# Hybrid encoder block on one core: the two last products with tokens on the partitions, x added as it lies, x2 turned at the second norm

## What is computed

```python
h_in = rms_norm(x, norm1_w)                 # x: (1, 512, 2048)
z = h_in @ w_in                             # attention, RWKV and gate columns
...                                         # o_attn (512 wide), o_rwkv (1024 wide), gates
branch_a = o_attn @ w_branch_attn
branch_b = o_rwkv @ w_branch_rwkv
merged = gates[:, :, 0] * branch_a + gates[:, :, 1] * branch_b
x = x + merged @ w_out                      # output projection and residual: "x2"
h = rms_norm(x, norm2_w)
x = x + (silu(h @ w_ffn_gate) * (h @ w_ffn_up)) @ w_ffn_down    # 5632 hidden channels
```

## Time and profile before

| | us |
|---|---|
| median of 3 runs | 3535.35 |
| lowest and highest run | 3525.96 and 3536.68 |
| the profiled execution | 3531.09 |
| its span in the trace | 3529.4 |
| TensorE busy | 3445.0 |
| VectorE, ScalarE, GpSimd busy | 1593.3, 1112.2, 1685.0 |

### The profile page before, as it was taken

How to read it: one execution, slowest core, us unless ns; L and a number is a source line. 1 busy time by engine, 2 the same in 40 slices (tenths; PEclk the granted TensorE clock), 3 DMA queues, 4 the chain that set the end, 5 groups by cost and what they waited for, 6 DMA issues and landing times.

```text
span 3529.4 us, 43830 instructions
## 1 busy us (share of the span) xinstructions
PE 3445.0 (98%) x16535; PEld 2803.1 (79%) x16535; DVE 1593.3 (45%) x1890; ACT 1112.2 (32%) x1757; POOL 1685.0 (48%) x1429
## 2 busy tenths in 40 slices
PE   8999999999999999999799999999999999999999
PEld 6777777777777888888578878888888888888887
DVE  4455545555567877874344443311331133203321
ACT  4333324444234554553342232211221222112211
POOL 4333333333338888887275434444444444344443
PEclk9999999999999999999899999999999999999999
DMA  6344434433354555553543423333332333333323
GB/s 193 108 137 123 131 116 145 118 113 91 96 154 119 129 127 146 126 133 89 205 138 113 121 88 95 95 90 112 95 95 83 108 95 96 90 103 100 99 85 105
DMA packets 757677, 406.25 MB, mean 115 GB/s; under 512 B 191695, under 2 KB 718219, under 8 KB 757035
## 3 DMA queue, kind: packets, MB, share of 16 engines
q1 hardware_dynamic: 757546, 404.53, 40.3%
HBM read 345.73 MB, written 58.72 MB: 115 GB/s over the span
## 4 chain that ended last, share of the span: by engine, by line
PE 50%; DVE 1%; ACT 0%; DMA 0%; POOL 0%; issue 0%; SPq 0%; DVEq 0%; ACTq 0%; POOLq 0%
PE f_bank L149 15%; PE f_bank L151 15%; PE f_bank L150 15%; PE f_bank L1865 1%; PE f_bank L1866 1%; PE f_bank L1867 1%; DMA act_plain<-yt 0%; PE f_bank L1898 0%; PE f_bank L1874 0%; POOL w_lo_b L140 0%; DVE hid_plain L2322 0%; ACT w_hi_b L133 0%; PE f_bank L1878 0%; DVE act_rounded L2276 0%; PE f_bank L1981 0%
## 5 line engine op out<-in xcount | busy, mean ns | idle before, releaser
L140 POOL TENSOR_TENSOR w_lo_b<-w_raw_b,w_hi_b 128x2048 fp32r<-128x2048 f32 (+1 forms) x168 | 684.7, 4076 | 925.0 <-ACT w_hi_b L133 925.0
L149 PE MATMUL f_bank<-act_rounded,w_lo_b 128*128 128x512 f32 x1664 | 648.6, 390 | 9.1 <-DVE act_rounded L2276 6.6
L150 PE MATMUL f_bank<-act_rounded,w_hi_b 128*128 128x512 f32 x1664 | 648.1, 389 | 0.0
L151 PE MATMUL f_bank<-act_rounded,w_hi_b 128*128 128x512 f32 x1664 | 647.9, 389 | 0.0
L1260 POOL TENSOR_TENSOR ring_w_rounded<-ring_w_plain,ring_w_hi 128x1024 fp32r<-128x1024 f32 x138 | 331.8, 2406 | 626.4 <-ACT ring_w_hi L1273 626.4
L133 ACT CAST w_hi_b<-w_raw_b 128x2048 fp32r<-128x2048 f32 (+1 forms) x168 | 286.4, 1705 | 838.3 <-PE f_bank L151 828.0
L1555 PE MATMUL slab_ps<-h_hi,ring_w_rounded 128*128 128x512 f32 x1088 | 451.4, 415 | 5.1 <-POOL ring_w_rounded L1260 2.6
L1557 PE MATMUL slab_ps<-h_hi,ring_w_hi 128*128 128x512 f32 x1088 | 426.2, 392 | 0.0
L1556 PE MATMUL slab_ps<-h_lo,ring_w_hi 128*128 128x512 f32 x1088 | 426.2, 392 | 0.0
L149 PEld LDWEIGHTS f_bank<-act_rounded,w_lo_b 128*128 128x128 f32 x1664 | 312.6, 188 | 75.4 <-DVE act_rounded L2276 5.3
L151 PEld LDWEIGHTS f_bank<-act_rounded,w_hi_b 128*128 128x128 f32 x1664 | 312.7, 188 | 65.3
(11 more groups left out here) (347 smaller groups left out, 5275.9 us busy)
## 6 DMA issues: line engine op xcount, KB each, us to landing
ring_w_plain<-in_w_in_dram SPq DMA_DIRECT2D x190, 512.0 KB, 4.1
w_raw_b<-in_w_ffn_gate_dram SPq DMA_DIRECT2D x44, 1024.0 KB, 5.2
w_raw_b<-in_w_ffn_up_dram SPq DMA_DIRECT2D x44, 1024.0 KB, 5.1
w_raw_b<-in_w_ffn_down_dram SPq DMA_DIRECT2D x64, 704.0 KB, 4.5
zt<-slab_out SPq DMA_DIRECT2D x65, 256.0 KB, 4.4
w_raw_b<-in_w_out_dram SPq DMA_DIRECT2D x16, 1024.0 KB, 5.5
zt<-lout SPq DMA_DIRECT2D x40, 256.0 KB, 4.6
b_in<-zt SPq DMA_DIRECT2D x80, 128.0 KB, 3.5
```

The lines of the kernel that those rows point to most:

```text
L140: pool.tensor_tensor(g.w_lo[n.slot][:, 0:k, :], g.w_raw[n.slot][:, 0:k, :], g.w_hi[n.slot][:, 0:k, :].bitcast(F32), ALU.subtract).then_inc ...
L149: pe.matmul(bank, wl, hi[:, ka, :], start=start and j == 0, stop=False)
L150: pe.matmul(bank, wh, lo[:, ka, :], start=False, stop=False)
L151: ins = pe.matmul(bank, wh, hi[:, ka, :], start=False, stop=stop and j == len(ks) - 1)
```

## The change

The output projection and the last product swap their operands: the activations (128 channels by 128 tokens) are stationary and the weights (128 by 512 columns) move, so that the result lies with tokens on the partitions. Four banks, one for each 128 tokens, fill together for a group of 512 columns. `outp(q)` counts 16 slabs as before, a slab now being 4 k tiles by 512 columns; `down(b, q)` counts ND = 12 pieces of 4, 4 and 3 k tiles by 512 columns for each of the 4 groups, in place of 16 slabs. Loads of weights have runs of 2 KB, where they had 512 bytes.

x2 is kept in the same buffer, read by `by_tokens(c, t)` as 128 tokens by 512 columns. x is added from eight buffers that SP fills from the input itself. xt, x_turned, `keep`, the 64 unscaled transposes, their copies, the stores and the waits on them are gone, and VectorE and ScalarE share the scaling of x_tok otherwise. The squares are summed by ScalarE along the row (accum_out), and the sum over channels by matmuls is gone. At the second norm TensorE turns x2 (`turn_x2`), four blocks to a tile, into banks 0 to 3: four tiles ahead of the first gate slab, the others between its steps; act_hi and act_lo are made from these banks. At the end x2 is stored as it lies, with no turn and no copy. The loops over slabs of the two products are written out.

```diff
@@ phase_project, SP @@
-                def keep(t):
-                    sp.wait_ge(raw_taken, 4 * t + 4)
-                    sp.dma_start(xt.rearrange("(k p) n -> p k n", p=P)[:, :, t * P:(t + 1) * P], x_turned[t][:, :, :]).then_inc(x_kept[t], 16)
...
-                for t in range(TT):
-                    keep(t)
                 for s in range(N_SLOT + 2):
                     weights(2 * s + 4)
@@ phase_project, ScalarE @@
                 def scale(t):
                     act.wait_ge(rstd_ready, t + 1)
-                    act.wait_ge(raw_turned, 4 * t + 4)
-                    act.activation(x_tok[:, t, D_MODEL // 2:D_MODEL], x_tok[:, t, D_MODEL // 2:D_MODEL], ACT.Copy, scale=rstd[:, t:t + 1]).then_inc(scaled_act, 1)
+                    act.activation(x_tok[:, t, 0:D_MODEL // 2], x_tok[:, t, 0:D_MODEL // 2], ACT.Copy, scale=rstd[:, t:t + 1]).then_inc(scaled_act, 1)
...
-                scale(2)
+                scale(3)
@@ phase_project, VectorE @@
-                scale(1)
-                scale(2)
-                mean_square(3)
-                scale(3)
+                for t in range(1, TT):
+                    mean_square(t)
+                    scale(t)
@@ phase_output, SP @@
+                for q in range(KD):
+                    n = outp(q)
+                    c, i = divmod(q, 4)
+                    sp.wait_ge(g.w_lo_ready, n.count(2))
+                    sp.dma_start(g.w_raw[n.slot][:, :, :].rearrange("p (k j) n -> p k (j n)", j=4),
+                                 w_o[:, 4 * i:4 * i + 4, c * SEQ:(c + 1) * SEQ]).then_inc(g.w_landed[n.slot], 16)
+                    if q == 1:
+                        for n in range(NX):
+                            x_load(n)
+                    elif i == 3 and 1 <= c < 3:
+                        for n in range(4 * c + 4, 4 * c + 8):
+                            x_load(n)
...
-                    sp.dma_start(out[0, t * P:(t + 1) * P, q * SEQ:(q + 1) * SEQ], plain[:, n, :]).then_inc(out_stored, 16)
+                    sp.wait_ge(x2_ready, KD + (NBLK - 1) * KD + n + 1)
+                    sp.dma_start(out[0, t * P:(t + 1) * P, c * SEQ:(c + 1) * SEQ].rearrange("p (m f) -> p m f", f=P), by_tokens(c, t)
+                                 ).then_inc(out_stored, 16)
@@ phase_output, TensorE @@
+                for q in range(KD):
+                    st = outp(q)
+                    c, i = divmod(q, 4)
+                    pe.wait_ge(g.w_lo_ready, st.count())
+                    for kk in range(4):
+                        k = 4 * i + kk
+                        if c == 0:
+                            pe.wait_ge(mlo_ready, k + 1)
+                        wh, wl = by_columns(g.w_hi, st, kk), by_columns(g.w_lo, st, kk)
+                        for t in range(TT):
+                            if k == 0 and c:
+                                pe.wait_ge(x2_ready, 4 * (c - 1) + t + 1)
+                            o, r = bank[4 + t][:, :], slice(t * P, (t + 1) * P)
+                            pe.matmul(o, act_hi[:, k, r], wl, start=k == 0, stop=False)
+                            pe.matmul(o, act_lo[:, k, r], wh, start=False, stop=False)
+                            ins = pe.matmul(o, act_hi[:, k, r], wh, start=False, stop=k == KD - 1)
...
+                for m in range(4):
+                    turn_x2(m)
                 st = gate_up(0, 0, 0)
                 pe.wait_ge(g.w_lo_ready, st.count())
                 for k in range(KD):
                     pe.wait_ge(h2lo_ready, k + 1)
                     ins = products(pe, g, st, [(k, k)], bank[6][:, :], act_hi, act_lo, start=k == 0, stop=k == KD - 1)
+                    if k + 4 < KD:
+                        turn_x2(k + 4)
                 ins.then_inc(g.w_used, 1)
-                pe.wait_ge(sq_added, KD)
-                for t in range(TT):
-                    ins = pe.matmul(bank[4][:, t:t + 1], sq_sum[:, t * P:(t + 1) * P], g.all_ones[:, 0:1], start=True, stop=True)
@@ phase_output, ScalarE @@
                 for k in range(KD):
-                    act.wait_ge(x2_ready, k + 1)
-                    act.activation(act_hi[:, k, :], x2[:, k, :], ACT.Copy, scale=param(g, "norm2", k)).then_inc(h2hi_ready, 1)
-                    if k == 3:
+                    act.wait_ge(turned, k + 1)
+                    act.activation(act_hi[:, k, :], bank[k % 4][:, :], ACT.Copy, scale=param(g, "norm2", k)).then_inc(h2hi_ready, 1)
+                    if k == 7:
                         split_hi(act, g, gate_up(0, 0, 1), KD)
+                    if k == 9:
+                        square_x2(3)
@@ phase_output, VectorE @@
-                    dve.scalar_tensor_tensor(out=act_lo[:, k, :], in0=x2[:, k, :], scalar=param(g, "norm2", k),
+                    dve.scalar_tensor_tensor(out=act_lo[:, k, :], in0=bank[k % 4][:, :], scalar=param(g, "norm2", k),
                                              in1=act_hi[:, k, :].bitcast(F32), op0=ALU.mult, op1=ALU.subtract).then_inc(h2lo_ready, 1)
```

More of the change, by code:

```diff
@@ L1903, in _ @@
                     branch_slab(m)
-                def slabs(step, first, freed, i, K, banks, hi, lo):
-                    for j in range(2):
-                        st = step(i, first + j)
-                        pe.wait_ge(g.w_lo_ready, st.count())
-                        if first:
-                            pe.wait_ge(freed, i * 2 + (j + 1))
-                        products(pe, g, st, [(k, k) for k in range(K)], bank[banks + j][:, :], hi, lo).then_inc(g.w_used, 1)
-                st = outp(0, 0)
@@ L1922, in _, with by_columns @@
-                pe.wait_ge(g.w_lo_ready, st.count())
-                products(pe, g, st, [(k, k) for k in range(KD)], bank[5][:, :], act_hi, act_lo).then_inc(g.w_used, 1)
-                with pe.Fori(0, KD // 2 - 1) as i:
-                    slabs(outp, 2, x2_ready, i, KD, 4, act_hi, act_lo)
+                def by_columns(w, st, i):
+                    return w[st.slot][:, 4 * i:4 * i + 4, :].rearrange("p j n -> p (j n)")
+                for q in range(KD):
[14 more added lines that the diff above has]
+                            ins = pe.matmul(o, act_hi[:, k, r], wh, start=False, stop=k == KD - 1)
+                            if k == KD - 1 and t < TT - 1:
+                                ins.then_inc(made_x2, 1)
+                    ins.then_inc(g.w_used, 1)
@@ L1926, in gate_slab, with turn_x2 @@
+                turn_bank = bank[0:4]
+                def turn_x2(m):
+                    if m % 4 == 0:
+                        pe.wait_ge(x2_ready, m + 4)
+                    if m >= 4:
+                        pe.wait_ge(h2lo_ready, m - 3)
+                    for t in range(TT):
+                        ins = pe.transpose(turn_bank[m % 4][:, t * P:(t + 1) * P], x2[:, m, t * P:(t + 1) * P], g.ident[:, :])
+                    ins.then_inc(turned, 1)
                 def gate_slab(b, i, j):
@@ L2163, in _ @@
                         split_lo(pool, g, gate_up(0, i, j + 2), KD)
-                with pool.Fori(0, KD // 2) as i:
-                    for j in range(2):
-                        split_lo(pool, g, down(0, i, j), HB)
+                for q in range(ND):
+                    split_lo(pool, g, down(0, q), 4 * len(piece(q)[1]))
                 with pool.Fori(0, NBLK - 1) as b1:
@@ L2171, in _ @@
                             split_lo(pool, g, gate_up(b, i, j), KD)
-                    with pool.Fori(0, KD // 2) as i:
-                        for j in range(2):
-                            split_lo(pool, g, down(b, i, j), HB)
+                    for q in range(ND):
+                        split_lo(pool, g, down(b, q), 4 * len(piece(q)[1]))
             @block.vector
@@ L2313, in _ @@
-                        dve.tensor_tensor(one(hid_lo[:, bass.ds(i, 1), :]), act_f, one(hid_hi[:, bass.ds(i, 1), :].bitcast(F32)),
-                                          ALU.subtract).then_inc(hlo_ready, 1)
-                    with dve.Fori(0, KD // 2) as i:
-                        for j in range(2):
-                            dve.wait_ge(g.w_used, down(b, i, j).count())
-                            x = one(x2[:, bass.ds(i * 2 + j, 1), :])
-                            dve.tensor_tensor(x, x, bank[j][:, :], ALU.add).then_inc(x2_ready, 1)
@@ L2320, in _ @@
-                for n in range(KD):
-                    dve.wait_ge(turned, n + 1)
-                    dve.tensor_copy(plain[:, n, :], bank[4 + n % 2][:, :]).then_inc(staged, 1)
+                        hidden(b, i)
+                    add_down(b)
 def build(nc, a, out):
@@ L2352, in build @@
             with nc.cleanup_on_exit():
[L2353 removed]
+                phase_project(nc, g, a, zt, oat)
             c0.close()
```

302 lines of the change are left out of this document (141 added, 161 removed).

## The result

| | us |
|---|---|
| changed kernel, median of 6 runs | 3508.55 (3505.26 to 3518.04) |
| kernel before, median of 6 runs | 3528.70 (3525.34 to 3536.68) |
| ratio | 0.9935, 95% interval 0.9919 to 0.9951 |
| profiled execution, changed and before | 3510.56 and 3531.09 |
| its span, changed and before | 3508.8 and 3529.4 |

A forecast was written before the change was run, and what follows sets the result against it. TensorE, busy 3445.0 of 3529.4 us, was taken as the bound, so only its work and idle time count. 2.9 + 2.6 - 1.6 + 11.0 = 14.9 us gave 3516.2 profiled, 3520.5 for the median; range 3508 to 3533.

The forecast's parts named there:

- The sum: Whole kernel: the gains and losses of all places added, 2.9 + 2.6 - 1.6 + 11.0 = 14.9 us gained.
- Start: Before the first projection: first matmul at 21.0 instead of 23.94, 2.9 us earlier; bounds 0 to 4.
- DRAM copy: Wait for weights at 60 to 70 us: without the copy's stores, weight loads go out sooner, 2.6 us gained; bounds 0 and 2.6.
- Rival (4): Removing the copy of x frees nothing, weights being late anyway; end stores take their upper price: 3524; chance 0.07.
- The two products: Output projection and last product: same matmul counts at 0.227 us each, bank hand-overs hidden, 0 us.
- Rival (2): In both turned products, the first matmul behind each bank change costs 0.33, not 0.23: 96 us slower, 3616; chance 0.05.
- rival (3): At 15 group hand-overs TensorE starves and drops to 1.2 GHz, 1.75 us each, 26 us: 3547; chance 0.04.
- Second norm: From projection end to third hidden slab: turning x2 on TensorE takes 36.7 against 35.05, 1.6 us lost; 2 gained to 8 lost.
- 1.39 us a step: At the second norm: price of four transposes plus three matmuls, read at the first norm; 12 steps 16.7 us.
- Rival (1): Gain given back at the second norm: steps slow as at the first, cast and squares unhidden; 3527.5; chance 0.20.
- The clock's part: At the old second norm: a granted clock of 0.95 over 35.05 us is 3.5 us at 1.2 GHz.
- Tail: After the last matmul: without the final turns and copies the end comes 11.0 us sooner; ends 9.8 and 12.1.

The follow-up runs named there:

- the stores late: Kernel before with its four stores of the turned x queued on SP behind the next four loads of weights, nothing else changed; ratio 0.9975 (0.9965 to 0.9985).

## Why the prediction was right in its direction and wrong in its size

**Where it starts from.** The first error is not in the kernel. The sum was subtracted from the median of 3 runs, 3535.35, with the argument that this median lay 4.3 us above the profiled execution. Six runs gave 3528.70, and 34 later ones 3533.3 at the median; the profiled execution, 3531.09, was as good a centre as any. 14.9 us below it is 3516.2. Against the median of the comparison, 3528.70, the figure of 3520.5 stood for only 8 us of gain, though the text forecast 14.9. A median of 3 with 11 us between its ends can't carry a correction of 4 us.

**Start.** Right: first matmul at 21.10 for 21.0, by the chain that was forecast, over ScalarE's half. The gain is 1.30 us of an earlier mean and 1.54 us between it and the first turn, where ScalarE's 1.15 us stands in place of VectorE's held 2.82.

**DRAM copy.** The mechanism was right, shown by the stores late. Rival (4), by which the weights would have been late anyway, is dead. Its size was read from the idle times in the earlier trace rows, 2.6 us, and is 3.1 to 3.3, by starts on both sides. An idle time in these rows begins at the end of a matmul, which lasts 0.39 where the next could start after 0.227; each of the two waits is longer by those 0.16. The remaining 0.2 to 0.4 the traces don't lay open. The clock behind the longer wait, which fell in one execution of five, had no term.

**The two products.** Right to 0.06 us of 1589. Rival (2) and rival (3) are dead: clock 1.00 and 0.227 us a matmul over 15 hand-overs and all changes of bank. What the prediction weighed from the Trainium skill (TensorE: Matmul & The Clock Gate, "A second HAM failure mode: psum-queue depth-cycling") did not occur: TensorE's waits show none at a hand-over.

**Second norm.** Here a term was mis-sized and changed its sign: -1.6 forecast, +1.4 measured. The step that failed is "1.39 us a step". It rightly left out the 0.23 us of wait before 46.58, but counted the four transposes at 0.60 us, from 45.76 to 46.35, and then the first matmul at 0.33 and two at 0.23. The 0.60 is a duration that runs past the start of the next instruction: from start to start they hold TensorE 0.35 us. Where nothing waits the step is 1.13 to 1.14 us: three matmuls 0.69, four transposes 0.35, and 0.1 for the first matmul behind them. Twelve steps at 0.25 less are 3.0 us, the whole miss. The rest of the working came out within 0.6 each: the eleventh step starts 0.99 us late where 0.4 of wait were forecast (its row says 0.73, by the same overlap), and from the second slab's start to the third's pass 14.1 us for 14.5. Rival (1) is dead with it. The clock's part was right: 1.00 over the stretch where it had been 0.95.

**Tail.** 11.8 for 11.0, inside its ends of 9.8 and 12.1.

**What no term had.** The clock outside the second norm. By the places that it touches the change gives 19.4 us in the profiled pair, of which the sum has 14.9. The timed runs say 20 by the medians and 23 by the ratio (17 to 29). Their mean clocks differ by what is worth 4.8 us, of which 2.4 to 3.6 lie outside the second norm, and the scan takes 2 to 3 back in the traces: an estimate of 19 to 21. The prediction had named the clock as a danger and, in the second norm, as part of the old time; that it would also be higher elsewhere stood in no term. How much of that the removed waits bring about is not shown. That the time lies inside the range at all is luck: its low end, 3508, was the best ends of the sum less 6.6 us for the spread of three runs.

## What to carry to other kernels

Take what an instruction holds an engine for from the distance between starts, never from its duration, where matmuls overlap: an error of 0.25 us in a step that occurs twelve times was larger than the term. Do the sum against the profiled execution unless many runs say otherwise. And where VectorE and GpSimd meet, letting another operation of the same chain meet the subtraction was worth nothing (4.93 for 4.91 us of wait). An operand in PSUM, another engine, or a start 0.3 us ahead of the subtraction freed VectorE here.

## What the runs showed of the hardware that was not expected

The granted clock falls behind the same wait of 1.1 us in some executions of a program and not in others, at 3 us each, and over the runs of one kernel 0.001 less of mean clock goes with 2.1 to 2.6 us more. Two profiled executions of the kernel before differ by 6 us (3529.4 and 3523.2): 3 at this place, 2.3 in branches and merge, 1.1 in the scan. Taking 3 us of waits out of the first 80 gave 7 to 9 us in timed runs (5 to 12 by the interval).

SP mostly needs 0.4 to 0.5 us to issue a DMA in the scan, but 1.2 to 2.6 at 11 to 16 places, most of which recur in executions of one kernel and shift with the first phase. What sets them stays open: it is not the number of SP's instructions ahead, and not the place of the stores in its queue.
